# Splitting the first loads, transposes and operand splits of a fused decoder kernel into single k-tiles

## The reference, cut to what matters

```
h    = rmsnorm(x) * norm_mix_g                 # x: 256 x 2048
proj = h @ w_in                                # w_in: 2048 x 8192
dq, dk, dv, mq, mk, mv, gate = split(proj)     # 8 + 8 heads of 128 columns, 2048 gate columns
y    = concat(diff_attention(dq, dk, dv), moba_attention(mq, mk, mv)) * silu(gate)
x    = x + y @ w_out                           # 2048 x 2048
q, (km, vm) = rmsnorm(x)*g @ w_q_mem, rmsnorm(mem)*g @ w_kv_mem
x    = x + attention(q, km, vm) @ w_o_mem
out  = rmsnorm(x) * final_g
```

## Time and profile before

| | |
|---|---|
| median of 3 runs | 594.91 us (594.54 to 594.98) |
| the profiled execution's own time | 594.71 us |
| its span in the profile | 592.9 us |
| PE (matmul) busy | 581.2 us, 98% |
| PE weight loads busy | 494.3 us, 83% |
| DVE busy | 429.5 us, 72% |
| ACT busy | 326.7 us, 55% |
| GpSimd busy | 36.3 us, 6% |
| moved by the loads' queue | 111.32 MB |

### The profile page before, as it was taken

The page is one execution under the profiler, slowest core; times in us unless marked ns, Lnnn a source line. Parts: engine busy times, 40 slices in busy tenths (PEclk is TensorE's granted clock), DMA queues, the critical chain, the costliest instruction groups (busy, mean ns, idle before and its releaser), DMA issues.

```text
span 592.9 us, 9278 instructions
## 1 busy us (share of the span) xinstructions
PE 581.2 (98%) x3022; PEld 494.3 (83%) x3022; DVE 429.5 (72%) x709; ACT 326.7 (55%) x549; POOL 36.3 (6%) x57
## 2 busy tenths in 40 slices
PE   8999999999999999999999999999999999999994
PEld 7888888888888888888888888888888888888883
DVE  4698879879879879577686676766566657655875
ACT  5766556546636735635654654553456665445723
POOL 2001101201200200200110110010000000000000
PEclk9999999999999999999999999999999999999998
DMA  8976745754755765655665565579554556454203
GB/s 279 325 259 199 231 142 169 221 189 146 230 184 165 177 217 178 203 191 166 189 190 172 182 203 177 179 202 335 184 174 159 180 180 203 171 189 143 107 2 142
DMA packets 104060, 111.66 MB, mean 188 GB/s; under 512 B 19761, under 2 KB 85858, under 8 KB 103522
## 3 DMA queue, kind: packets, MB, share of 16 engines
q1 hardware_dynamic: 104002, 111.32, 58.2%
q10 hardware_dynamic: 32, 0.01, 0.0%
HBM read 106.06 MB, written 2.10 MB: 182 GB/s over the span
## 4 chain that ended last, share of the span: by engine, by line
PE 96%; ACT 1%; DVE 1%; DMA 1%; issue 0%; SPq 0%; ACTq 0%; DVEq 0%
PE ps L536 19%; PE ps L487 19%; PE ps L489 18%; PE ps L488 18%; PE ps L544 10%; PE ps L578 2%; PE ps L518 2%; PE ps L740 1%; PE ps L736 1%; PE ps L735 1%; PE ps L559 1%; DMA xs<-in_x 1%; PE ps L709 1%; PE ps L585 1%; PE ps L689 1%
## 5 line engine op out<-in xcount | busy, mean ns | idle before, releaser
L994 DVE TENSOR_TENSOR w_lo<-w_raw,w_hi 128x1024 fp32r<-128x1024 f32 x187 | 228.5, 1226 | 104.8 <-ACT w_hi L771 103.2
L771 ACT ACTIVATE w_hi<-w_raw 128x1024 fp32r<-128x1024 f32 x187 | 198.0, 1060 | 157.2 <-PE ps L489 79.1
L536 PE MATMUL ps<-aT,w_hi 128*128 128x512 f32 x512 | 140.6, 396 | 0.0
L487 PE MATMUL ps<-w_hi,aT 128*128 128x512 f32 x320 | 126.9, 397 | 0.0
L488 PE MATMUL ps<-w_lo,aT 128*128 128x512 f32 x320 | 125.0, 391 | 0.0
L489 PE MATMUL ps<-w_hi,aT 128*128 128x512 f32 x320 | 124.9, 390 | 0.0
L536 PEld LDWEIGHTS ps<-aT,w_hi 128*128 128x128 f32 x512 | 88.0, 189 | 12.2 <-issue 0.2
L544 PEld LDWEIGHTS ps<-aT,w_lo 128*128 128x128 f32 x512 | 78.5, 189 | 10.8
L544 PE MATMUL ps<-aT,w_lo 128*128 128x256 f32 x512 | 81.4, 281 | 0.0
L489 PEld LDWEIGHTS ps<-w_hi,aT 128*128 128x128 f32 x320 | 60.1, 188 | 12.8
L487 PEld LDWEIGHTS ps<-w_hi,aT 128*128 128x128 f32 x320 | 60.2, 188 | 12.0
(11 more groups left out here) (167 smaller groups left out, 566.4 us busy)
## 6 DMA issues: line engine op xcount, KB each, us to landing
w_raw<-in_w_in SPq DMA_DIRECT2D x256, 256.0 KB, 2.8
w_raw<-in_w_out SPq DMA_DIRECT2D x64, 256.0 KB, 3.4
w_raw<-in_w_kv_mem SPq DMA_DIRECT2D x32, 256.0 KB, 2.9
w_raw<-in_w_q_mem SPq DMA_DIRECT2D x16, 256.0 KB, 2.8
w_raw<-in_w_o_mem SPq DMA_DIRECT2D x16, 256.0 KB, 3.2
mems<-in_mem SPq DMA_DIRECT2D x1, 2048.0 KB, 9.5
xs<-in_x SPq DMA_DIRECT2D x3, 512.0 KB, 7.2
w_raw<-in_final_g SPq DMA_DIRECT2D x1, 1024.0 KB, 4.9
```

The lines of the kernel that those rows point to most:

```text
L487: pe.matmul(acc, hi[:, k0 + k, tok], w_hi[:, slot, k], start=first and k == 0, stop=False)
L536: pe.matmul(ps[:, c, :], w_hi[:, slot, k, c * P:(c + 1) * P], aT[:, k0 + k].rearrange("p i s -> p (i s)"), start=first and k == 0, stop=False)
L771: act.activation(w_hi[:, i % SPLITS], raw, ACT.Copy).then_inc(hi_made, 1)
L994: dve.tensor_tensor(lo, w_raw[:, i % RAW], hi.bitcast(F32), ALU.subtract).then_inc(lo_made, 1)
```

## The change

The first two halves and the first two blocks of x are loaded, transposed and split in smaller pieces, and PE's order around them is new:

- Loads. x comes in seven parts instead of five: k-tiles 0 and 1 alone (128 columns, 128 KB each), then three of 256 columns, then two of 512. Halves 0 and 1 come k-tile by k-tile: k-tile 0 in one load of 256 KB (both slabs of columns), k-tile 1 in two of 128 KB. The new order is x0, half 0 k0, x1, half 0 k1, x2, half 1 k0, half 1 k1, x3, half 2, x4, half 3, x5, halves 4 and 5, x6.
- PE. `WARM_UP` goes from (5, 4, 2) to (3, 4). k-tile 0 of x is transposed alone into bank 6, then four unneeded products, then k-tile 1 into bank 4 (`transpose_first`). Then half 0's k-tile 0, the transposes of bank (0,1), half 0's k-tile 1, half 1's k-tile 0, bank (1,0), half 1's k-tile 1, bank (1,1), half 2. From there on the order is as before.
- ACT and DVE. Both take k-tile 0 of x, k-tile 0 of half 0, k-tile 1 of x, k-tile 1 of half 0, then bank (0,1), half 1 k-tile by k-tile, bank (1,0), half 2, bank (1,1), as before.

```diff
-X_PARTS = ((0, 256), (256, 512), (512, 1024), (1024, 1536), (1536, 2048))
-WARM_UP = (5, 4, 2)
+X_PARTS = ((0, 128), (128, 256), (256, 512), (512, 768), (768, 1024), (1024, 1536), (1536, 2048))
+X_PART_OF = {(1, 0): 3, (1, 1): 4, (2, 0): 5, (3, 0): 6}
+WARM_UP = (3, 4)
...
+            def load_pair_rows(n, k):
+                if k == 0:
+                    sp.dma_start(w_raw[:, n, 0, :].rearrange("p (s c) -> p s c", c=2 * P),
+                                 in_slabs[n][:, 0, 0:2, 0:2 * P]).then_inc(k_loaded[n], 16)
+                else:
+                    for part, slab in enumerate(SLABS["diff", 0]):
+                        sp.dma_start(w_raw[:, n, 1, part * 2 * P:(part + 1) * 2 * P], in_slabs[n][:, 1, slab, 0:2 * P]
+                                     ).then_inc(half_loaded[n], 16)
             load_x(0)
-            for n in range(PAIR_HALVES):
+            for n in range(2):
+                load_pair_rows(n, 0)
+                if n == 0:
+                    load_x(1)
+                load_pair_rows(n, 1)
+                load_x(2 + n)
+            for n in range(2, PAIR_HALVES):
                 load_pair_half(DIFF, 0, 0, n)
-                if n in (0, 1, 3, 5):
-                    load_x((n + 1) // 2 + 1)
+                if n in (2, 3, 5):
+                    load_x({2: 4, 3: 5, 5: 6}[n])
...
+            def transpose_first(k):
+                pe.wait_ge(x_loaded[k], 16)
+                for t in range(NT):
+                    m = pe.transpose(ps[:, 6 - 2 * k, (k * NT + t) * P:(k * NT + t + 1) * P],
+                                     xs[:, t, k * P:(k + 1) * P], ident[:, :])
+                m.then_inc(k_made if k == 0 else block_made, 1)
...
             def project_qk(half, slot, k0, first, last):
...
+                early = half if isinstance(half, int) and half < 2 else None
+                if early is None:
                     wait(pe, lo_made, half + 1)
                 for k in range(GK // 2):
+                    if early is not None and k == 0:
+                        if early == 0:
+                            pe.wait_ge(k_block_lo, 1)
+                        pe.wait_ge(k_hi, early + 1)
+                    if early is not None and k == 1:
+                        pe.wait_ge(block_lo, early + 1)
+                        pe.wait_ge(hi_made, early + 1)
...
+                    if early is not None and k == 0:
+                        transpose_block(early, (1 - early,))
...
-                        if n in (0, 2, 4):
+                        if n == 1:
+                            transpose_block(1, (1,))
+                        if n in (2, 4):
                             transpose_block(1 + n // 2)
...
-            transpose_block(0)
+            transpose_first(0)
+            keep_busy(WARM_UP[1])
+            transpose_first(1)
...
+                if isinstance(half, int) and half < 2:
+                    act.wait_ge(k_loaded[half], 16)
+                    act.activation(w_hi[:, half, 0], raw[:, 0], ACT.Copy).then_inc(k_hi, 1)
+                    if half == 0:
+                        block_hi_first(1)
+                    act.wait_ge(half_loaded[half], 32)
+                    act.activation(w_hi[:, half, 1], raw[:, 1], ACT.Copy).then_inc(hi_made, 1)
+                    return
```

More of the change, by code:

```diff
@@ L254, in program @@
         half_loaded = [sem(f"half_loaded{s}") for s in range(RAW)]
-        first_hi = sem("first_hi")
-        first_lo = sem("first_lo")
+        k_loaded = [sem("k_loaded0"), sem("k_loaded1")]
+        k_made = sem("k_made")
+        k_block_hi = sem("k_block_hi")
+        k_block_lo = sem("k_block_lo")
+        k_hi = sem("k_hi")
+        k_lo = sem("k_lo")
         hi_made = sem("hi_made")
@@ L473, in half_group @@
             def half_group(half, slot, banks, hi, lo, k0, first, last):
[L476 to L480, removed]
+                wait(pe, lo_made, half + 1)
                 for k in range(GK // 2):
-                    if first_half and k == 1:
-                        pe.wait_ge(lo_made, 1)
                     for t in range(NT):
@@ L497, in keep_busy, with transpose_block @@
                     pe.matmul(ps[:, 2, 0:P], ident[:, :], ident[:, :], start=True, stop=True)
-            def transpose_block(b):
+            def transpose_first(k):
[4 more added lines that the diff above has]
+                m.then_inc(k_made if k == 0 else block_made, 1)
+            def transpose_block(b, banks=(0, 1)):
                 source, n, bank = BLOCKS[b]
@@ L503, in transpose_block @@
                 before = [c for c in range(b) if BLOCKS[c][2] == bank]
-                if source == "x" and n > 0:
-                    pe.wait_ge(x_loaded[n + 1], 16)
                 if source == "mem":
@@ L511, in transpose_block @@
                     pe.wait_ge(block_lo, 2 * (before[-1] + 1))
-                for i in range(2):
+                for i in banks:
+                    if (n, i) in X_PART_OF and source == "x":
+                        pe.wait_ge(x_loaded[X_PART_OF[n, i]], 16)
                     if source == "x" and n == 0:
-                        pe.wait_ge(x_loaded[i], 16)
+                        pe.wait_ge(x_loaded[2], 16)
                     for k in range(2):
@@ L520, in transpose_block @@
                     m.then_inc(block_made, 1)
-                    if source == "x" and n == 0:
-                        keep_busy(WARM_UP[1 + i])
             def project_qk(half, slot, k0, first, last):
[L527 to L530, removed]
+                early = half if isinstance(half, int) and half < 2 else None
+                if early is None:
                     wait(pe, lo_made, half + 1)
                 for k in range(GK // 2):
-                    if first_half and k == 1:
-                        pe.wait_ge(hi_made, 1)
+                    if early is not None and k == 0:
[5 more added lines that the diff above has]
+                        pe.wait_ge(hi_made, early + 1)
                     for c in range(4):
@@ L537, in project_qk @@
                                   aT[:, k0 + k].rearrange("p i s -> p (i s)"), start=first and k == 0, stop=False)
-                    if first_half:
+                    if early is not None:
                         if k == 0:
-                            pe.wait_ge(first_lo, 1)
+                            pe.wait_ge(k_lo, early + 1)
                         else:
-                            pe.wait_ge(lo_made, 1)
+                            pe.wait_ge(lo_made, early + 1)
                     for c in range(4):
@@ L599, in pair_window @@
                     if n < PAIR_HALVES // 2:
-                        if first:
+                        if first and n > 0:
                             pe.wait_ge(block_lo, n + 1)
@@ L756, in split_hi @@
             def split_hi(half, i, turn, tail=False):
+                raw = w_raw[:, i % RAW]
+                if isinstance(half, int) and half < 2:
[6 more added lines that the diff above has]
+                    return
                 act.wait_ge(half_loaded[i % RAW], 32 * (turn + i // RAW + 1))
-                raw = w_raw[:, i % RAW]
                 if tail and i in range(WO_HALF0, WO_HALF0 + SPLITS):
@@ L765, in split_hi, with block_hi_first @@
                 wait(act, half_done, half - behind + 1)
[L766 to L770, removed]
                 act.activation(w_hi[:, i % SPLITS], raw, ACT.Copy).then_inc(hi_made, 1)
+            def block_hi_first(k):
+                if k == 0:
+                    act.wait_ge(k_made, 1)
+                else:
+                    act.wait_ge(block_made, 1)
+                act.activation(aT_hi[:, k], ps[:, 6 - 2 * k, k * SEQ:(k + 1) * SEQ], ACT.Identity,
+                               scale=gainsT[:, k:k + 1]).then_inc(k_block_hi if k == 0 else block_hi, 1)
             def block_hi_bank(b, i):
@@ L859, in _ @@
             act.wait_ge(gainsT_ready, 1)
-            block_hi_bank(0, 0)
+            block_hi_first(0)
             split_hi(0, 0, 0)
@@ L983, in split_lo @@
                 lo = wo_lo[:, i - WO_HALF0] if over_yT else w_lo[:, i % SPLITS]
[L984 to L990, removed]
+                if isinstance(half, int) and half < 2:
+                    dve.wait_ge(k_hi, half + 1)
+                    dve.tensor_tensor(lo[:, 0], w_raw[:, half, 0], hi[:, 0].bitcast(F32), ALU.subtract
+                                      ).then_inc(k_lo, 1)
+                    if half == 0:
+                        block_lo_first(1)
+                    dve.wait_ge(hi_made, half + 1)
+                    dve.tensor_tensor(lo[:, 1], w_raw[:, half, 1], hi[:, 1].bitcast(F32), ALU.subtract
                                       ).then_inc(lo_made, 1)
@@ L994, in split_lo, with block_lo_first @@
                 dve.tensor_tensor(lo, w_raw[:, i % RAW], hi.bitcast(F32), ALU.subtract).then_inc(lo_made, 1)
+            def block_lo_first(k):
+                if k == 0:
+                    dve.wait_ge(k_block_hi, 1)
+                else:
```

(6 more changed lines are left out.)

## The result

The changed kernel takes **596.03 us** (median of 20 runs, 595.42 to 597.02) against 594.67 us (20 runs, 594.26 to 595.26). The ratio is 1.0023, 95% interval 1.0016 to 1.0029: 1.4 us slower. The prediction said 595.2 in a range of 593.8 to 596.8. The time lies in the range, and the direction of the forecast (+0.3) was right, but the loss is four times the 0.33 us of the sum and, at 0.23%, just past what I had called no change (0.2%), so it falls to the chance of 0.19 that I gave to a slower kernel.

A forecast was written before the change was run, and what follows sets the result against it. PE was taken to bound the kernel, busy 98% of the span, with gains possible only at the start. Half 2 at 7.5 + 7.80 = 15.30 instead of 14.97 gave +0.33 us, 595.0; the median's extra 0.2 made 595.2, range 593.8 to 596.8.

The forecast's parts named there:

- the 0.33 us of the sum: Whole kernel: half 2 at 15.30 us instead of 14.97, everything behind shifting with it, so +0.33 us.
- the chance of 0.19 that I gave to a slower kernel: Whole kernel: 0.19 for a measurably slower time, with late x2 at 0.12 and the slow clock at 0.07.
- The saving of 2.3 us ends at two waits: PE's start: products at 6.0 instead of 8.27, then waits of about 0.7 us before half 1 and 1.6 before half 2.
- A: Start of PE's transposes of bank (0,1), at 7.40 us before the change.
- From A to half 2: 7.80 us: From bank (0,1)'s transposes to half 2's products: 7.80 us expected, against 7.57 before.
- The lost cover of 0.23 us: Bank (0,1): half 0 no longer covers ACT's and DVE's work on it, at a cost of 0.23 us.
- A = 7.5: Bank (0,1)'s transposes start at 7.5 us: x2 landing at 7.45 plus 0.05 for smaller runs.
- Landing by bytes: x2's load: it comes by its bytes, in ring order, at about 7.4 us.
- time from issue: x2's load: counted from its issue it would land at 9.3 us and the total be 596.9.
- PE at full pace at 6.0: First products: k-tile 0 takes 1.4 us; the slow-pace rival (0.07) said 2.8 and a total of 596.4 to 596.6.
- Behind half 2 everything shifts alike; half 7's load has slack: Behind half 2: order unchanged, work shifts with PE; half 7's last load has slack 0.45 us and 0.3 more, extra load time 0.
- the forecast's own bin: Whole kernel: A from 7.3 to 8.3 and total 594.7 to 596.0 us, chance 0.66.

The follow-up runs named there:

- a_turn10: The changed kernel with PE's transposes of bank (1,0) moved ahead of half 1's k-tile 0; 595.35 us against 594.80 before (1.0013).
- a_half2: The changed kernel with ACT and DVE taking half 2's split ahead of bank (1,0), PE unchanged; 595.59 us (1.0014 against before).
- b_xl: The kernel before with only its first x load cut into columns 0 to 127 and 128 to 255; 595.54 us against 594.69 (1.0016).
- a_merge34: The changed kernel with x's columns 512 to 1023 in one load again; 595.68 us against 594.84 before (1.0014).
- a_again: The changed kernel unedited, measured and traced again; 595.85 us against 594.69 before (1.0019).
- b_wl: The kernel before with only halves 0 and 1 loaded by k-tiles; 594.92 us against 594.69 (1.0007).
- a_nofill: The changed kernel without the four unneeded products between the transposes of k-tiles 0 and 1; 596.13 us (1.0022 against before).
- b_best: The kernel before without fillers ahead of half 0, lambda loads behind half 7's, half 7's split ahead of bank (3,0); 593.74 us against 594.69 (0.9986).

## Why the prediction was right or wrong

- *The saving of 2.3 us ends at two waits.* Right, shown by the first trace and by a_turn10 and a_half2, which each took one link out of the chain and moved half 2 by what was left. First products at 6.00 (6.0 expected), waits of 0.44 and 1.39 us (0.7 and 1.6; the working's own terms add up to A + 6.28 for PE and so to 1.5).
- *From A to half 2: 7.80 us.* Right: 7.86, 7.81 and 7.77 in the three traces, against 7.57 before. The lost cover of 0.23 us is there.
- *A = 7.5.* **This is the term that was mis-sized**: 7.78, 8.03 and 8.36. Two causes. The first is the landing of x2, taken at 7.45, and 7.76, 7.96 and 7.6 in the three traces; it set A in the first two. I took one landing of before (7.37) for a constant, where the same loads gave 6.8 to 7.4, and had allowed 0.05 for the smaller runs; with the new loads it was 6.9 to 8.0. The second cause is the pace of PE, the next point. Landing by bytes served better than time from issue, which gave 9.3. That agrees with the ring order that the Trainium skill states ("DMA: Bandwidth & Descriptors", section "Queues, rings and completion order"). The Trainium skill has runs of 512 bytes at line rate (same page, section "Specifications"). No trace separates a rate for such runs, but a kernel that differs only by them and one more load, b_xl, was 0.85 us above before (0.2 to 1.6).
- *PE at full pace at 6.0.* This is the step that failed, in some executions and not in others; it was a rival with a chance of 0.07. Four first products took 1.89 us or more in three of the seven traces that keep the changed kernel's start and its fillers (a_half2, a_merge34, a_again), 1.44 and 1.54 in two, and were at full pace in two. Before, a rise that late did little harm, because the products began at 8.27 (0.24 us in b_wl). The change moved them into the time in which the pace differs from one execution to the next. I priced this at +1.4 us at A, but only what exceeds the wait for x2 is paid: 8.36 - 7.6 = 0.8 in a_again. a_nofill, with fewer products and a gap of 0.98 us, had the longest slow stretch from the start, up to 9.2 us. The Trainium skill ("TensorE: Matmul & The Clock Gate", Part 1) has the slow clock as the default that activity releases, which agrees.
- *Behind half 2 everything shifts alike; half 7's load has slack.* True for the unedited change (half 2 +0.67, pair 1 +0.68), by luck, since its own lateness hid the later loads: the last load of half 7 came at 17.88 + 8.5 = 26.4, 1.1 us later than in the earlier trace rows, and ACT took it at 26.42. So the slack was gone, where I had taken the extra load time as 0. (I had also written that 0.9 us of it would leave 0.2; against a slack of 0.45 + 0.33 it leaves 0.1.) Had the PE order brought its 2.3 us, the loads of halves 6 and 7 would have taken most of them: in a_turn10 they took 1.4 of 1.76.
- *The size of the loss.* A at 8.36 gives 595.9, A at 7.78 gives 595.4. So x2's landing put A at 7.8 to 8.0 and the pace at up to 8.4. The median of 596.03 of the first 20 runs would be A at 8.5, which no trace of this code shows. The highest of those runs, 597.02, has no trace; a late x2 followed by half pace, as in b_xl's, would do it, but that is only argued. That the time lies in the stated range owes much to the width of the range: the forecast's own bin ended at 596.0.

## What to carry to other kernels

A handover by smaller pieces helps only the engine that waits for the first piece. Follow the earlier start to the point where the next full-size step joins (here 11.8 us, with a rigid chain of 3.83 us behind it), and ask what covered that step before. Before putting real products where fillers stood, look at the pace of the rows there: work moved into the slow stretch takes up to 1.7 times as long (2.04 us instead of 1.18). Take a landing time from more than one trace: the same load came at 6.8, 7.1 and 7.4 us. And look for the floor one stage on: of b_best's 0.89 us, 0.60 lay in what ACT waits for and does 10 to 15 us later.

## What the runs showed of the hardware that I had not expected

- The time at which PE goes to full pace varies between executions of the same code: four products at 6.00 us took 1.18, 1.44 and 2.04 us. In b_xl PE was at full pace early (eight fillers in 1.06 us at 5.22), and after a gap of 2.04 us it was at half pace again: four products at 9.78 us took 2.05 us.
- The landing of one and the same early load varies between executions: x2, asked for at 2.27 us, landed at 6.8, 7.1 and 7.4 us.
- In the one trace with an early 256 KB load cut into two of 128 KB with 512-byte runs, the load that stands three loads further on landed 0.9 us later, 0.5 of it because it was issued later.
- With all the new loads the DMA engines moved 247 to 295 GB/s at 10 to 12 us in eight traces, instead of 369 to 379 in three traces with the old ones, in a stretch whose packets averaged 1 KB in both.
